# Two-layer hybrid trunk with grouped experts: TensorE filler products before and between turned blocks, and parameter rows loaded from SyncE's queue

## What is computed

```python
def reference(x, ...):
    h = layer_norm(x, ln_in_g, ln_in_b)
    for l in range(DEPTH):                       # DEPTH = 2
        mix = hybrid_mixer(h, w_in[l], w_out[l], ...)
        h = layer_norm(DEEPNORM_ALPHA * h + mix, ln_mix_g[l], ln_mix_b[l])
        ffn = grouped_moe(h, w_router, router_bias, w_gate[l], w_up[l], w_down[l])
        h = layer_norm(DEEPNORM_ALPHA * h + ffn, ln_ffn_g[l], ln_ffn_b[l])
    return h
```

```python
y = (jax.nn.silu(hf @ w_gate[e]) * (hf @ w_up[e])) @ w_down[e]
out = out + gates[:, e:e + 1] * y
```

## Time and profile before

| What | Value |
|---|---|
| Median of 3 runs | 727.23 us (725.63 to 731.33) |
| Profiled execution | 731.4 us |
| Its span, first to last instruction | 729.5 us |
| TensorE busy | 670.5 us (92%) |
| VectorE busy | 281.0 us (39%) |
| ScalarE busy | 141.6 us (19%) |
| GpSimd busy | 67.9 us (9%) |
| Moved by DMA | 240.70 MB, mean 330 GB/s |
| Mean granted TensorE clock | 0.974 |

### The profile page before, as it was taken

How to read it: one execution, slowest core, us unless ns; L and a number is a source line. 1 busy time by engine, 2 the same in 40 slices (tenths; PEclk the granted TensorE clock), 3 DMA queues, 4 the chain that set the end, 5 groups by cost and what they waited for, 6 DMA issues and landing times.

```text
span 729.5 us, 7323 instructions
## 1 busy us (share of the span) xinstructions
PE 670.5 (92%) x3009; PEld 331.4 (45%) x3009; DVE 281.0 (39%) x585; ACT 141.6 (19%) x280; POOL 67.9 (9%) x65
## 2 busy tenths in 40 slices
PE   4999998999999999887789999989999999997882
PEld 3645587543333543232375446855333345332331
DVE  4396767410323122120626946771120330320326
ACT  3102453221110221110121026522201113110100
POOL 1603000320000000000050220006000000000000
PEclk9999999799999999999969999999999999999997
DMA  9999636089999999999999441433999999999981
GB/s 282 336 388 416 249 116 231 1 342 414 422 421 420 423 422 420 422 421 422 392 386 408 187 184 56 159 134 127 381 422 422 420 420 423 420 420 422 421 364 59
DMA packets 48571, 240.70 MB, mean 330 GB/s; under 512 B 4428, under 2 KB 8852, under 8 KB 23956
## 3 DMA queue, kind: packets, MB, share of 16 engines
q1 hardware_dynamic: 47380, 235.97, 80.6%
q10 hardware_dynamic: 1152, 4.19, 1.4%
HBM read 239.10 MB, written 1.05 MB: 329 GB/s over the span
## 4 chain that ended last, share of the span: by engine, by line
PE 73%; DMA 18%; DVE 6%; issue 1%; ACT 1%; POOL 0%; DVEq 0%
PE bank L534 21%; PE bank L455 15%; PE bank L553 12%; DMA ring<-in_w_up 9%; DMA ring<-in_w_gate 8%; PE bank L469 5%; PE bank L512 5%; PE bank L614 4%; PE bank L573 3%; PE bank L433 1%; PE bank L425 1%; PE bank L542 1%; PE bank L686 1%; DVE stats L1204 1%; DVE h L1197 1%
## 5 line engine op out<-in xcount | busy, mean ns | idle before, releaser
L534 PE MATMUL bank<-ring,xe 128*64 128x512 f32 x1024 | 226.3, 594 | 18.2 <-DMA ring<-in_w_up 10.4
L534 PEld LDWEIGHTS bank<-ring,xe 128*64 128x64 f32 x1024 | 71.5, 137 | 166.3 <-issue 134.5
L553 PE MATMUL bank<-ring,area_b 128*64 128x512 f32 x512 | 113.4, 595 | 1.6 <-DVE area_b L1218 1.6
L455 PE MATMUL bank<-ring,xT_area 128*128 128x512 f32 x256 | 111.3, 593 | 0.0
L1212 DVE TENSOR_TENSOR area_b<-area_b,bank 128x512 f32<-128x512 f32 x16 | 11.0, 688 | 257.3 <-PE bank L534 257.3
L455 PEld LDWEIGHTS bank<-ring,xT_area 128*128 128x128 f32 x256 | 48.1, 190 | 57.4 <-issue 57.4
L553 PEld LDWEIGHTS bank<-ring,area_b 128*64 128x64 f32 x512 | 35.3, 137 | 68.3 <-issue 64.0
L937 POOL TENSOR_TENSOR rstd<-var_eps,half_neg 128x1 f32<-128x1 f32 x18 | 11.7, 658 | 548.9 <-DVE var_eps L1024 548.9
L1232 DVE SCALAR_TENSOR_TENSOR y_lo<-bank,slot_gate,y_hi 128x512 fp32r<-128x512 f32 x32 | 24.0, 751 | 89.1 <-ACT y_hi L858 89.1
L1280 DVE SCALAR_TENSOR_TENSOR mix<-glu,tapsT,mix 128x256 f32<-128x256 f32 x120 | 47.7, 479 | 0.0
L858 ACT ACTIVATE y_hi<-bank,slot_gate 128x512 fp32r<-128x512 f32 x32 | 22.0, 687 | 98.0 <-PE bank L553 98.0
(11 more groups left out here) (159 smaller groups left out, 589.0 us busy)
## 6 DMA issues: line engine op xcount, KB each, us to landing
ring<-in_w_gate SPq DMA_DIRECT2D x32, 2048.0 KB, 23.3
ring<-in_w_up SPq DMA_DIRECT2D x32, 2048.0 KB, 24.4
ring<-in_w_down SPq DMA_DIRECT2D x32, 2048.0 KB, 26.3
ring<-in_w_in SPq DMA_DIRECT2D x9, 2048.0 KB, 21.2
ring<-in_w_out SPq DMA_DIRECT2D x4, 2048.0 KB, 20.6
ring<-in_w_in SPq DMA_DIRECT2D x2, 1024.0 KB, 7.1
h<-in_x SPq DMA_DIRECT2D x2, 512.0 KB, 4.2
ln_par<-in_ln_mix_g ACTq DMA_DIRECT2D x2, 512.0 KB, 8.0
```

Source lines behind the costliest of these rows:

```text
L455: mm = pe.matmul(dst[:, :], xT[:, c, b * P:(b + 1) * P], w[:, c, :], start=c == 0, stop=c == KC - 1)
L534: mm = pe.matmul(bank[2 + u % 2][e * SLOTS:(e + 1) * SLOTS, :], xe[:, k, at + e * SLOTS:at + (e + 1) * SLOTS], w[:, e, c, :], start=k == 0 ...
L553: mm = pe.matmul(bank[5 + n][e * SLOTS:(e + 1) * SLOTS, :], hidT[:, k, e * SLOTS:(e + 1) * SLOTS], w[:, e, c, n * BANK:(n + 1) * BANK], st ...
```

## The change

Three things are changed. TensorE gets 18 fillers ahead of the first transposes of the kernel (bank 5), and six in each layer between the first turned block of the router and the products on it (bank 2). The two rows of the LayerNorm behind the experts are no longer loaded by ScalarE at the first pair of experts but by SyncE: those of layer 0 behind slab 0 of layer 1, those of layer 1 behind the last unit of all. ScalarE keeps the wait on `h_ready` that stood ahead of its two loads.

```diff
-KEEP_ROUTER, KEEP_SLOTS = 18, 6
+KEEP_START, KEEP_MIX, KEEP_ROUTER, KEEP_SLOTS = 18, 6, 18, 6
...
+            def load_ffn_rows(l):
+
+                sp.wait_ge(h_ready, 2 * TB * (l + 1))
+                sp.dma_start(ln_par[:, 0, :], bcast_row(ln_ffn_g[l], D)).then_inc(par_in, 16)
+                sp.dma_start(ln_par[:, 1, :], bcast_row(ln_ffn_b[l], D)).then_inc(par_in, 16)
+
             for l in range(DEPTH):
                 main, more = passes[l]
                 for i in range(SLABS):
                     load_slab(l, i, l * LAYER_UNITS + i)
+                    if l and i == 0:
+                        load_ffn_rows(l - 1)
...
                 load_pairs(l, main, PAIRS, 0, 0)
+                if l == DEPTH - 1:
+                    load_ffn_rows(l)
...
             pe.wait_ge(pool_const, 4)
+            keep_clock(5, KEEP_START)
             pe.wait_ge(table_in, 16)
...
                     turn(normal, b)
                     if b == 0 and l == 0:
                         shift_strips()
+                    if b == 0:
+                        keep_clock(2, KEEP_MIX)
                     wait_xT(l, 2, b)
...
                     if ps.main and j == 0:
-                        next_params(ln_ffn_g[l], ln_ffn_b[l], 2 * TB * (l + 1))
+                        act.wait_ge(h_ready, 2 * TB * (l + 1))
```

## The result

The changed kernel takes 721.62 us (median of 6 runs, 719.3 to 723.96) against 728.43 us for the kernel before (6 runs, 725.63 to 733.77): 6.8 us less, a ratio of 0.9905 with a 95% interval of 0.9877 to 0.9934. That is faster, clear of the noise, by slightly less than 1%. Forecast were 718.2 us (range 714 to 723), 9.0 us under the kernel before. The profiled execution took 721.64 us, span 719.8, where before it took 731.4, span 729.5: 9.7 us less in span.

What follows compares the result with a forecast made beforehand. Bound: the experts' DMA stream, begun when TensorE frees ring slots, then TensorE's clock dips. Rows 4.8, block fillers 2.2 and 1.05, start 1.0 sum to 9.05, say 9.0 us: median 727.23 to 718.2 us, range 714 to 723.

Steps and rivals of the forecast that it cites:

- The line of 1%: Whole kernel: 719.96 us, about 7.3 us faster, as what a measurement can tell from no change; 0.74 for below it.
- the last line of the sum: Whole kernel: profiled 731.4 us becomes 722.4; the median, 4.2 us lower, becomes 718.2 us.
- Rival 1: Start and routers: the clock costs more in ordinary runs than in the profiled one; gain 12.9, 714.3 us; chance 0.20.
- Block fillers: Routers: six fillers behind the first turned block keep the clock high, gaining 2.2 us in layer 0, 1.05 in layer 1.
- Start fillers: Kernel start: 18 fillers raise the clock before the first 16 transposes, gaining 1.0 us, bounds -0.5 to +4.0.
- The upper bound of +4.0: Kernel start: if the clock is ordinarily not up at 13.95 us, L614 pays 3.04 us that fillers would save.
- rival 2: Start and routers: the clock falls all the same despite fillers; gain only 4.8, 722.4 us; chance 0.14.
- Rows: Experts' DMA stream: moving 1.05 MB of LayerNorm rows from its head gains 2.4 us a layer, 4.8 together.
- The queue stays fed, barely: Experts' stream, layer 0: without the rows, units run dry at about 169 us; the next is issued at 167.25.
- waits for gate and up units down to about 13 us: Experts: sign of being right, TensorE's waits for these weight units falling from 18.1 to about 13 us.
- At no cost: ScalarE's two fewer issues counted as nothing; layer 0's rows land with 4 us to spare, later slabs come as before.

Runs made afterwards that it cites:

- rows twice: Kernel before with both LayerNorm rows loaded once more at the third pair of experts of each layer: 734.06 us, ratio 1.0088.
- the 24 fillers: Changed kernel with 24 more fillers ahead of layer 1's first turned block: 727.67 us; with 26 at the start as well, 727.48 us.
- with 24 fillers: Changed kernel with 26 fillers at the start and 24 ahead of TensorE's branch after layer 0: 723.25 us, ratio 0.9924.
- with 10: Changed kernel with 26 fillers at the start and 10 ahead of TensorE's branch after layer 0: 721.80 us, ratio 0.9913.
- 26 fillers: Changed kernel with 26 instead of 18 fillers at the start, here also 24 ahead of TensorE's branch after layer 0: 723.25 us, ratio 0.9924.

## Why the prediction was right or wrong

**The range and the direction held**; the gain was forecast at 9.0 us and is 6.8. The line of 1% was not reached: 721.62 us lies above 719.96, and the prediction had given 0.74 to a time below it.

**The step that failed is the last line of the sum**, "the median of 727.23 is 4.2 us lower, and I take the same difference off it". Against its own execution the sum was close: 9.05 forecast, 9.7 measured in span, of which 1.5 is luck in layer 1; it had 722.4 us for the changed kernel's execution, and that took 721.64. But the difference that it took off belongs to the kernel before alone: its execution lies 3.0 us over the median of six runs (4.2 over that of the first three), the changed kernel's 0.0 over its own. That execution of before wasn't like the median. In 35 runs of the kernel before the mean granted clock falls into three groups, and the time goes with it:

| Mean clock | Runs | Median us |
|---|---|---|
| 0.988 to 0.989 | 12 | 726.8 |
| 0.980 to 0.981 | 20 | 729.5 |
| 0.974 | 3 | 731.1 |

In the 38 further runs beside the later experiments the first two groups lie only 1.0 and 1.6 us apart, and three runs had 0.974, at 731 to 734 us. The profiled execution had 0.974 and 731.4 us. It had a dip in both routers and a long one in layer 1. A third of the runs were at 0.988 or more already, about the best that the changed kernel reaches, so the fillers had little to save in them: those twelve runs have a median of 726.8 us, the kernel with both kinds of fillers 725.9. The mean of the changed kernel's six is 0.986, and its runs spread over 4.7 us where those of before spread over 8.1. Rival 1, to which I gave 0.20, had the sign wrong: ordinary runs lose less to the clock than this one did, not more. That the moment at which the clock rises differs from run to run is what the Trainium skill says (TensorE: Matmul & The Clock Gate, Part 1: The HAM clock gate), and the traces agree: the same 18 fillers at the start take between 5.44 and 6.67 us. L614 of layer 1 took anything from 14.05 to 17.09 us in traces of kernels with nothing changed near it. The prediction cited the rule and then drew on it for the start alone.

**Block fillers** (2.2 and 1.05 us). Right to 0.15 us for a run in which the clock falls: 16.60 to 14.25 and 15.00 to 13.96. What the sum had no term for is a run in which it doesn't. The trace with the rows twice has a router 0 of 13.95 us without fillers, 0.3 *shorter* than the 14.25 with them, since the fillers hold the first product on xT back: it starts 2.83 us behind the start of the first transposes in the changed kernel, 2.35 without fillers. In layer 1, where they fit the wait, 13.95 and 13.96 are the same. Over the four traces without them, router 0 fell into the low clock three times and router 1 twice; at these shares the fillers are worth 0.75 x 2.35 - 0.25 x 0.3 + 0.5 x 1.04 = 2.2 us, an estimate from few traces, and alone they measured 1.7 (0.3 to 3.1).

**Start fillers** (1.0 us). Right in the trace, 1.2 us. The end of the fillers was taken at 8.0 us and is 6.75 here, as they run at the higher clock sooner; in the six traces with 18 it lies between 6.75 and 7.98. The upper bound of +4.0 rested on a slow L614 in ordinary runs of before; in all four traces without these fillers it took 14.05 us at the start. The low clock behind the start came with the fillers, in two of ten traces, at 1.7 us each: something like rival 2 at the start, but behind the transposes and not on them, and whether the fillers caused it is not shown. Alone they measured 2.9 us (1.5 to 4.4), more than any trace explains.

**Rows** (4.8 us). The mechanism was right, the size somewhat too large: 2.1 us in layer 0 and 1.9 in layer 1 over the traces, 4.0 together. 1.05 MB does cost 2.5 us in the middle of the stream (rows twice), but at its head, where the rows stood, the queue has barely more in it than it moves. "The queue stays fed, barely" was the place: it doesn't. The reckoning had 1.75 us between the next unit's issue and the moment at which the queue would be empty, and took that for enough. But the first unit of the same stream, issued at 142.71 us, moves 74 GB/s in the microsecond from 143, 246 from 144 and 401 from 145: more than 2 us until it flows in full. The sign that was named for this term, waits for gate and up units down to about 13 us, came only in part: 14.9.

**At no cost** stood ScalarE's issues, the rows' landing and the slabs behind them; all three held. In layer 0 the rows were 5 us early, and in layer 1 VectorE reads the tile at 711.6 us with no wait ahead of it.

**The wait at the start of layer 1** has no term in the sum, and no part of the change depends on it.

4.0 for the rows, 2.2 for the block fillers and 0.8 for the start (1.1 by the mean starts, less two falls in ten at 1.7) make 7.0 us, against 6.8 measured. That the two are so close is in part luck: these are prices from traces, put together afterwards, and the medians of the parts alone read 5.0, 1.7 and 2.9.

## What to carry to other kernels

Before an estimate goes from a profiled execution to the median, ask which of several kinds of run it was: the mean granted clock of each run tells it here. A filler pays only where TensorE waits in all runs and the clock falls in some, and what is longer than the wait is paid in the runs where the clock doesn't fall. A load costs its bytes only where the queue behind it is full; at the head of a stream, look at the next issue. A wait that the profile puts down to another engine may be TensorE's own, when the gap is nearly the same in every trace; then look when the named engine was ready, since only the time between that and the end of the wait can be won.

## What the runs showed of the hardware

- TensorE stands idle for some 5.5 us between layers (5.53 to 5.62 in the twelve traces without fillers ahead of its branch, among them the 5.56 and 5.57 "issue" of the 24 fillers): a branch that isn't taken, over two nested loops of the experts' products, seems to cost that; no run leaves it out. It hides some work that is already in the queue: 3.4 of 5.4 us with 24 fillers, all but 0.1 to 0.2 of 2.3 with 10.
- The granted clock fell in the midst of steady work: in the start-only kernel from 12.6 to 15.9 us, while L621 ran, after fillers, a wait of 1.1 us, transposes at the high clock and a wait of 1.7 us. A second trace has such a fall (26 fillers, no wait ahead of the transposes, 1.97 us behind them, L625 at 15.74 us); eight traces with fillers at the start, with waits of the same lengths, have none. What decides is not shown.
- The time of the kernel before goes with the mean granted clock over runs of one program: 726.8 us at 0.988, 729.5 at 0.981 and 731.1 at 0.974 in 35 runs, with 1.0 to 1.6 us between the first two in 38 others.
